# Tokens of experts 1 to 7 fetched by an indirect DMA and turned by transposes, in place of a gather by 0/1 products

## Chip, cores and metric

The kernel runs on one core of one Trainium2 chip. The metric is the device time of one execution in microseconds, lower is better. A comparison is made between medians of runs.

## What is computed

A two-layer decoder trunk on 256 tokens of width 1024, in float32. Layer 0 has two groups of sparse attention heads and a dense SwiGLU, layer 1 has stick-breaking attention and a top-2-of-8 expert SwiGLU. The part around the change is the last one:

```
logits = h @ w_router                       # h: 256 x 1024, normed tokens
top_v, top_i = top_k(logits, 2); top_w = softmax(top_v)
gates = sum(one_hot(top_i, 8) * top_w)      # 256 x 8, two non-zero a row
for e in range(8):                          # w_gate, w_up: 1024 x 3584, w_down: 3584 x 1024
    y = y + gates[:, e] * ((silu(h @ w_gate[e]) * (h @ w_up[e])) @ w_down[e])
```

All three matrices of all eight experts are read, 42 blocks of 1 MB for an expert, 336 in all.

## The kernel before

**Weights as a stream of units.** A unit is 1 MB of weights, 128 partitions x 2048 floats. SyncE loads units in a fixed order into a ring `raw` of R = 6 slots (L549), each load waiting until VectorE has finished with the slot's former unit (`lo_ready`). ScalarE copies a unit to `hi` in fp32r (L632), VectorE makes `lo = raw - hi` (L975), and TensorE takes each product three times, hi*hi, hi*lo and lo*hi (`three`, L1442 to L1444, 12 matmuls of 512 columns a unit). `hi` and `lo` have HM = 4 slots in the expert stage; ScalarE waits for `units_used` of TensorE to reuse one.

**Routing.** After the last norm (L997 writes the normed tokens into `work[:, 0:2]`), the router's logits are formed and VectorE finds each token's two experts. `rplace` is a token's place among the tokens of an expert, `rpick` says whether it was chosen. If no expert has over 128 tokens (`few`, read by each engine from `most_i`), the branch followed here runs; else a dense one over all tokens.

**Expert loop.** `make_place(e)` on VectorE (L1285) makes `place`, two 128x128 matrices (256 tokens in T = 2 blocks by 128 places) with a one where a token has a place. `gather(e)` on TensorE (L1837) forms the tokens of the expert with features on the partitions: for each of KD = 8 blocks of 128 features, four products of a block of the tokens (`xs_hi` and `xs_lo`, two blocks of tokens) with `place`, so 32 matmuls of 128 columns, into PSUM banks 4 and 5. ScalarE and VectorE copy them to `xg_hi` (L862) and `xg_lo` (L1294). `transpose_place(e)` (L1916) turns `place` for the scatter; ScalarE copies that to `placeT` (L905), and VectorE may then make the next `place`.

**Order within an expert**, as TensorE runs it (numbers are units, g, u and d are gate, up and down, c the chunk): g0 (0, 1), u0 (2, 3), g1 (4 to 7), u1 (8 to 11), d0 (12, 13), `transpose_place`, g2 (14 to 17), u2 (18 to 21), d1 (22 to 25), g3 (26 to 29), u3 (30 to 33), d2 (34 to 37), `gather(e + 1)`, d3 (38 to 41). Between them stand groups of four transposes of the hidden activations (`g_transpose_h`, L1908), whose input has a step of four floats, and the four scatter products of the expert before (L1853, L1854), into PSUM bank 6. Two such groups of transposes lie inside g2 and at its end, the seventh right behind `gather(e + 1)`. ScalarE's and VectorE's orders are written out to match, with splits of units ahead of what TensorE needs (to three units on ScalarE, two on VectorE). `few`, `gather` and the loop are printed below.

GpSimd makes constants at the start, applies masks in the attention stages and issues the loads of the norm gains (L598 to L602). It has no work after 478 us of the profile.

Of the kernel before, what the change touches and what calls it, by code (L numbers as in the profile page):

```python
# [20 lines left out]
F32 = mybir.dt.float32  # L21
# [5 lines left out]
P = 128  # L27
SEQ = 256
D = 1024
KD = D // P  # L30
T = SEQ // P
# [103 lines left out]
def build(nc, x_d, rel_bias, ev_norm_mix, ev_w_in, ev_kv_norm, ev_w_uk, ev_w_uv, ev_cmp_pos, ev_cmp_w1,  # L135
# [86 lines left out]
    buckets_d = nc.inline_tensor(bucket_rows(), "bucket_rows").ap()  # L222
    diag_d = nc.dram_tensor("bias_by_distance", [CH, SEQ + P], F32).ap()

    with ExitStack() as ctx:
        def sb(name, shape, dt=F32):
            return ctx.enter_context(nc.sbuf_tensor(name, shape, dt))

        def sem(name):
            return ctx.enter_context(nc.semaphore(name))  # L230
# [70 lines left out]
        before = sb("before", [P, P])  # L301
        place = sb("place", [P, T, P], F32R)
        placeT = sb("placeT", [P, SEQ], F32R)
        ones = sb("ones", [P, SEQ])
        root = sb("root", [P, 1])
        idle_sb = sb("idle_sb", [P, W], F32R)
# [25 lines left out]
        hd = nc.alloc_sbuf_tensor_at("hd", [P, T, D], F32, offset=arena_at)  # L332
        y_hi, y_lo = (h[:, 4:8, :].rearrange("p a s -> p (a s)") for h in (xT_hi, xT_lo))
        topw = kv[:, 0:SEQ]
        hankel = work[:, 2:4, :].rearrange("p a (b s) -> p (a b) s", s=SEQ)


# [83 lines left out]
        places_done = sem("places_done")  # L421
        count_ready = sem("count_ready")
        place_ready = sem("place_ready")
        gathered = sem("gathered")
        xg_hi_ready = sem("xg_hi_ready")
        xg_ready = sem("xg_ready")
# [134 lines left out]
        @block.gpsimd  # L561
        def _(pool):
            pool.memset(ident[:], 0.0).then_inc(ident_ready, 1)
            pool.memset(flip[:], 0.0).then_inc(flip_ready, 1)
            pool.wait_ge(ident_ready, 1)
            pool.affine_select(out=ident[:], in_=ident[:], compare_op=ALU.not_equal, fill=1.0, base=0,
                               pattern=[[-1, P]], channel_multiplier=1).then_inc(ident_ready, 1)
            pool.wait_ge(flip_ready, 1)
            pool.affine_select(out=flip[:], in_=flip[:], compare_op=ALU.not_equal, fill=1.0, base=-(P - 1),
                               pattern=[[1, P]], channel_multiplier=1).then_inc(flip_ready, 1)  # L570
            pool.iota(iota[:], [[1, P]], base=0, channel_multiplier=0, allow_small_or_imprecise_dtypes=True)\
                .then_inc(iota_ready, 1)
            pool.memset(before[:], 1.0).then_inc(iota_ready, 1)
            pool.wait_ge(iota_ready, 2)
            pool.affine_select(out=before[:], in_=before[:], compare_op=ALU.is_gt, fill=0.0, base=0,
                               pattern=[[1, P]], channel_multiplier=-1).then_inc(iota_ready, 1)

            pool.wait_ge(diag_copied, 1)
            pool.dma_start(diag_d, diag_sb[:]).then_inc(diag_stored, 16)
            pool.wait_ge(diag_stored, 16)  # L580
            pool.dma_start(hankel, bass.AP(tensor=diag_d.tensor, offset=diag_d.offset,
                                           ap=[[1, P], [SEQ + P, CH], [1, SEQ]])).then_inc(hankel_loaded, 16)

            pool.wait_ge(bias_copied, 4)
            pool.affine_select(out=bias_kT[:], in_=bias_kT[:], compare_op=ALU.is_ge, fill=NEG, base=P,
                               pattern=[[0, 8], [-1, SEQ]], channel_multiplier=1).then_inc(bias_masked, 1)

            pool.wait_ge(gates_ready, 1)
            pool.affine_select(out=gates[:, 0, 0:BH], in_=gates[:, 0, 0:BH], compare_op=ALU.is_ge, fill=0.0,
                               base=-(CMP_LEN - 1), pattern=[[0, BH]], channel_multiplier=1)\  # L590
                .then_inc(gates_masked, 1)
            for i, t in enumerate((1, 0)):
                pool.wait_ge(idx_summed, i + 1)
                n = P * (t + 1)
                pool.affine_select(out=iscore[:, t, 0:n], in_=iscore[:, t, 0:n], compare_op=ALU.is_ge, fill=UNSEEN,
                                   base=P * t, pattern=[[-1, n]], channel_multiplier=1).then_inc(idx_masked, 1)
            pool.wait_ge(xs_ready, 2)
            pool.dma_start(gain[:, 0, :], row_to_all(gains[2])).then_inc(gain_loaded[2], 16)  # L598
            pool.wait_ge(xs_ready, 4)
            pool.dma_start(gain[:, 1, :], row_to_all(gains[3])).then_inc(gain_loaded[3], 16)  # L600
            pool.wait_ge(xs_ready, 6)
            pool.dma_start(gain[:, 0, :], row_to_all(gains[4])).then_inc(gain_loaded[4], 16)  # L602


            for b in range(NSTICK + 1):
                if b < NSTICK:
                    n = P * (STICK[b][0] + 1)
                    pool.wait_ge(rest_ready, b + 1)
                    lt = logit_tile(b, n)[:, :, n - P:n]
                    pool.affine_select(out=lt, in_=lt, compare_op=ALU.is_gt, fill=1.0, base=0,  # L610
                                       pattern=[[0, 4], [-1, P]], channel_multiplier=1).then_inc(rest_masked, 1)
                if b:
                    n = P * (STICK[b - 1][0] + 1)
                    pool.wait_ge(sticks_done, b)
                    pt = prob_tile(b - 1, n)[:, :, n - P:n]
                    pool.affine_select(out=pt, in_=pt, compare_op=ALU.is_gt, fill=0.0, base=0,
                                       pattern=[[0, 4], [-1, P]], channel_multiplier=1).then_inc(stick_masked, 1)


        @block.scalar  # L620
        def _(act):
# [257 lines left out]
            def g_hT_high(e, s):  # L879
# [2 lines left out]
                act.activation(hT_hi[:, :, hT_slot(NSUB * e + s)], ps[:, 7, :].rearrange("p (j q) -> p j q", q=P),  # L882
                               ACT.Copy).then_inc(g_hT_hi_ready, 1)

            fits = few(act)
            with act.If(fits):
                done[0] = U_MOE + HM
# [74 lines left out]
        def _(dve):  # L962
# [362 lines left out]
                dve.tensor_tensor(hT_lo[:, :, dst], ps[:, 7, :].rearrange("p (j q) -> p j q", q=P),  # L1325
                                  hT_hi[:, :, dst].bitcast(F32), ALU.subtract).then_inc(g_hT_ready, 1)

            dve.wait_ge(iota_ready, 3)
            make_place(0)
            splits_to(U_MOE + HM)  # L1330
            fits = few(dve)
            with dve.If(fits):
                done[0] = U_MOE + HM
                gathered_low(0)
                for e in range(NE):
                    def used(k):

                        splits_to(min(first_of(e) + k + 2, U_END))

                    if e:  # L1340
                        used(0)
                        y_low(e - 1)
                    used(GATE_AT[1])
                    multiply(e, 0)
                    if e:
                        add_scattered(0, e - 1)
                    used(GATE_AT[1] + 2)
                    g_hT_low(e, 0)
                    if e:
                        add_scattered(1, e - 1)  # L1350
                    used(UP_AT[1])
                    if e:
                        add_scattered(2, e - 1)
                    used(UP_AT[1] + 2)
                    if e:
                        add_scattered(3, e - 1)
                    used(DOWN_AT[0])
                    multiply(e, 1)
                    used(GATE_AT[2])
                    if e + 1 < NE:  # L1360
                        dve.wait_ge(placeT_done, e + 1)
                        make_place(e + 1)
                    used(GATE_AT[2] + 2)
                    g_hT_low(e, 1)
                    used(UP_AT[2])
                    g_hT_low(e, 2)
                    used(DOWN_AT[1])
                    multiply(e, 2)
                    used(GATE_AT[3] + 2)
                    g_hT_low(e, 3)  # L1370
                    used(UP_AT[3])
                    g_hT_low(e, 4)
                    used(DOWN_AT[2])
                    multiply(e, 3)
                    used(DOWN_AT[2] + 2)
                    g_hT_low(e, 5)
                    used(DOWN_AT[3])
                    if e + 1 < NE:
                        gathered_low(e + 1)
                    g_hT_low(e, 6)  # L1380
# [55 lines left out]
        def _(pe):  # L1436
# [378 lines left out]

            keep_busy(14, 5)
            pe.wait_ge(picks_ready, 2)
            pe.wait_ge(iota_ready, 3)
            pk = [rpick[:, t, 0:NE] for t in range(T)]
            pe.matmul(ps[:, 4, 16:24], before[:], pk[0], start=True, stop=True)  # L1820
            pe.matmul(ps[:, 4, 24:32], before[:], pk[1], start=True, stop=False)
# [3 lines left out]

            def gather(e):

                pe.wait_ge(place_ready, e + 1)
                if e == 0:
                    pe.wait_ge(xs_lo_ready, 1)  # L1830
                else:
                    pe.wait_ge(g_silu_done, NCH * e)
                for k in range(KD):
                    out = ps[:, 4 + k // 4, P * (k % 4):P * (k % 4) + P]
                    for t in range(T):
# [75 lines left out]
            def transpose_place(e):  # L1911
# [4 lines left out]
                    ins = pe.transpose(ps[:, 6, P * t:P * t + P], place[:, t, :].bitcast(F32), ident[:])  # L1916
                ins.then_inc(placeT_done, 1)

            gather(0)
            keep_busy(22, 7)  # L1920
            fits = few(pe)
            with pe.If(fits):
                for e in range(NE):
# [19 lines left out]
                    g_transpose_h(e, 1, 1)  # L1943
                    gate(e, 2, 2, 3)
                    g_transpose_h(e, 2, 1)
                    up(e, 2, 0, 1, 2, 3)
                    down(e, 1, 0, 1, 2, 3)
                    gate(e, 3, 0, 1)
# [94 lines left out]
```

## Time and profile before

| | us |
|---|---|
| median of 3 runs | 1540.04 (1537.26 to 1540.17) |
| profiled execution, its own time | 1536.09 |
| its span, first to last instruction | 1534.3 |
| TensorE busy in the span | 1485.8 (97%) |
| VectorE busy | 1137.9 (74%) |
| ScalarE busy | 938.2 (61%) |
| GpSimd busy | 13.2 (1%) |
| mean granted clock of TensorE | 0.988 |

Busy times overlap between engines; an engine's idle time matters only where another that sets the end waits for it. The profiled execution is 3.95 us under the median and 1.8 us over its own span.

### The profile page before, as it was taken

How to read it: one execution, taken by the hardware profiler on the slowest of the kernel's cores; microseconds unless marked ns; L12 is line 12 of the kernel's file. 1: busy time of each engine (PE TensorE's matmuls, PEld its weight loads, DVE VectorE, ACT ScalarE, POOL GpSimd, SP SyncE). 2: the span in 40 equal slices, each digit the busy share in tenths (PEclk: the TensorE clock that was granted, in tenths of full speed). 3: DMA queues.
4: the chain of work that ended last, by engine and by line, in shares of the span. 5: the costliest groups of instructions: out<-in, count | busy, mean ns of one | idle time of the engine just before them, and what ended most of it. 6: DMA issues, size and time to landing. Idle time of an engine off the chain costs nothing.

```text
span 1534.3 us, 17550 instructions
## 1 busy us (share of the span) xinstructions
PE 1485.8 (97%) x7359; PEld 1252.5 (82%) x7359; DVE 1137.9 (74%) x841; ACT 938.2 (61%) x727; POOL 13.2 (1%) x28
## 2 busy tenths in 40 slices
PE   8998999999999799999999999999999999999996
PEld 7895788888887688888888888888888888888885
DVE  4586544544454688899888888889889979988885
ACT  4544344334343477777777767766767777776773
POOL 0000000000000000000000000000000000000000
PEclk9998999999999899999999999999999999999998
DMA  9732255563543379999999999999999999999991
GB/s 317 211 122 82 98 181 174 185 201 116 188 147 111 110 290 364 340 366 362 365 340 356 381 334 363 372 334 361 379 333 358 370 366 344 353 375 340 358 373 81
DMA packets 127603, 429.74 MB, mean 280 GB/s; under 512 B 11064, under 2 KB 20256, under 8 KB 111776
## 3 DMA queue, kind: packets, MB, share of 16 engines
q1 hardware_dynamic: 124320, 424.24, 76.6%
q0 software_dynamic: 736, 2.63, 0.5%
q10 hardware_dynamic: 2464, 1.69, 0.4%
q8 instruction: 60, 0.98, 0.3%
q14 instruction: 23, 0.19, 0.0%
HBM read 427.48 MB, written 1.06 MB: 279 GB/s over the span
## 4 chain that ended last, share of the span: by engine, by line
PE 91%; DVE 5%; ACT 2%; issue 1%; DMA 0%; POOL 0%; DVEq 0%; ACTq 0%; POOLq 0%
PE ps L1442 28%; PE ps L1444 28%; PE ps L1443 28%; PE ps L1837 2%; PE ps L1908 2%; DVE lo L975 1%; PE ps L1655 1%; DVE work L997 1%; PE ps L1501 1%; DMA x<-in_x_dram 0%; DVE kv L1054 0%; PE ps L1853 0%; ACT hi L632 0%; PE ps L1854 0%; DVE top L1053 0%
## 5 line engine op out<-in xcount | busy, mean ns | idle before, releaser
L975 DVE TENSOR_TENSOR lo<-raw,hi 128x2048 fp32r<-128x2048 f32 (+1 forms) x403 | 903.0, 2284 | 129.6 <-ACT hi L632 128.2
L632 ACT ACTIVATE hi<-raw 128x2048 fp32r<-128x2048 f32 (+1 forms) x403 | 770.5, 1915 | 282.1 <-PE ps L1444 276.9
L1442 PE MATMUL ps<-hi,xT_hi 128*128 128x512 f32 (+2 forms) x1216 | 473.4, 389 | 4.0 <-DVE xT_lo L1128 1.9
L1444 PE MATMUL ps<-hi,xT_lo 128*128 128x512 f32 (+2 forms) x1216 | 468.3, 385 | 0.0
L1443 PE MATMUL ps<-lo,xT_hi 128*128 128x512 f32 (+2 forms) x1216 | 467.9, 385 | 0.0
L1442 PEld LDWEIGHTS ps<-hi,xT_hi 128*128 128x128 f32 x1216 | 229.0, 188 | 49.7 <-issue 2.4
L1444 PEld LDWEIGHTS ps<-hi,xT_lo 128*128 128x128 f32 x1216 | 228.4, 188 | 46.6
L1443 PEld LDWEIGHTS ps<-lo,xT_hi 128*128 128x128 f32 x1216 | 228.7, 188 | 44.0
L1442 PE MATMUL ps<-hi,hT_hi 128*128 128x512 f32 x536 | 210.2, 392 | 0.9 <-DVE hT_lo L1178 0.9
L1444 PE MATMUL ps<-hi,hT_lo 128*128 128x512 f32 x536 | 208.8, 390 | 0.0
L1443 PE MATMUL ps<-lo,hT_hi 128*128 128x512 f32 x536 | 208.6, 389 | 0.0
L1442 PEld LDWEIGHTS ps<-hi,hT_hi 128*128 128x128 f32 x536 | 100.8, 188 | 21.5 <-DVE hT_lo L1178 1.1
L1444 PEld LDWEIGHTS ps<-hi,hT_lo 128*128 128x128 f32 x536 | 100.6, 188 | 21.1
L1443 PEld LDWEIGHTS ps<-lo,hT_hi 128*128 128x128 f32 x536 | 100.7, 188 | 20.4
L1325 DVE TENSOR_TENSOR hT_lo<-ps,hT_hi 128x512 fp32r<-128x512 f32 x56 | 38.7, 690 | 69.5 <-ACT hT_hi L882 69.5
L1442 PE MATMUL ps<-xT_hi,hi 128*128 128x256 f32 x248 | 71.3, 288 | 2.7 <-DVE xT_lo L1005 2.7
L1443 PE MATMUL ps<-xT_lo,hi 128*128 128x256 f32 x248 | 70.9, 286 | 0.0
L1444 PE MATMUL ps<-xT_hi,lo 128*128 128x256 f32 x248 | 70.8, 286 | 0.0
L882 ACT ACTIVATE hT_hi<-ps 128x512 fp32r<-128x512 f32 x56 | 33.4, 597 | 40.1 <-PE ps L1908 40.1
L1442 PEld LDWEIGHTS ps<-xT_hi,hi 128*128 128x128 f32 x248 | 48.2, 194 | 3.8 <-issue 3.6
L1444 PEld LDWEIGHTS ps<-xT_hi,lo 128*128 128x128 f32 x248 | 48.3, 195 | 0.0
L1443 PEld LDWEIGHTS ps<-xT_lo,hi 128*128 128x128 f32 x248 | 48.2, 194 | 0.0
(235 smaller groups left out, 932.7 us busy)
## 6 DMA issues: line engine op xcount, KB each, us to landing
raw<-in_od_w_gate_dram SPq DMA_DIRECT2D x112, 1024.0 KB, 7.3
raw<-in_od_w_up_dram SPq DMA_DIRECT2D x112, 1024.0 KB, 7.4
raw<-in_od_w_down_dram SPq DMA_DIRECT2D x112, 1024.0 KB, 7.4
raw<-in_od_w_qkv_dram SPq DMA_DIRECT2D x12, 1024.0 KB, 5.3
raw<-in_ev_w_gate_dram SPq DMA_DIRECT2D x11, 1024.0 KB, 6.2
raw<-in_ev_w_up_dram SPq DMA_DIRECT2D x11, 1024.0 KB, 5.1
raw<-in_ev_w_down_dram SPq DMA_DIRECT2D x11, 1024.0 KB, 5.1
raw<-in_ev_w_in_dram SPq DMA_DIRECT2D x4, 1024.0 KB, 10.5
```

The lines of the kernel that those rows point to most:

```text
L632: act.activation(unit(hi, n), unit(raw, n), ACT.Copy).then_inc(hi_ready, 1)
L882: act.activation(hT_hi[:, :, hT_slot(NSUB * e + s)], ps[:, 7, :].rearrange("p (j q) -> p j q", q=P), ACT.Copy).then_inc(g_hT_hi_ready, 1)
L975: dve.tensor_tensor(unit(lo, n), unit(raw, n), unit(hi, n).bitcast(F32), ALU.subtract)\
L997: dve.scalar_tensor_tensor(out=work[:, t, :], in0=x[:, t, :], scalar=stat[:, 2 + t:3 + t], in1=gain[:, i % 2, :], op0=ALU.mult, op1=ALU.mult)\
L1325: dve.tensor_tensor(hT_lo[:, :, dst], ps[:, 7, :].rearrange("p (j q) -> p j q", q=P), hT_hi[:, :, dst].bitcast(F32), ALU.subtract).then_in ...
L1442: pe.matmul(out, s_hi, m_hi, start=start, stop=False, skip_group_check=True)
L1443: pe.matmul(out, s_hi, m_lo, start=False, stop=False, skip_group_check=True)
L1444: return pe.matmul(out, s_lo, m_hi, start=False, stop=stop, skip_group_check=True)
L1501: pe.matmul(ps[:, bank, :], idle_sb[:, 0:P], idle_sb[:], start=True, stop=True)
L1655: ins = pe.matmul(ps[:, 6 + g % 2, :], val, probT[0:m, c].rearrange("p h q -> p (h q)"), start=(first and c == 0), stop=closes(b), skip_gr ...
L1837: ins = pe.matmul(out, part[:, t, P * k:P * k + P], place[:, t, :], start=(t == 0 and part is xs_hi), stop=(t == T - 1 and part is xs_lo))
L1908: ins = pe.transpose(ps[:, 7, P * j:P * j + P], work[:, 1, f + j:f + W:4], ident[:])
```

## The change

The normed tokens are stored once to DRAM (`normed_d`, 256 x 1024) from GpSimd's queue. For each expert from 1 to 7, TensorE multiplies `place` with a column of token numbers (two float32 products with one column), which gives the number of the token that has each place; VectorE copies these 128 numbers as integers to `picked`; GpSimd issues an indirect DMA that fetches the 128 rows of 4 KB into `rows`, which is `work[:, 2]`; and `gather(e)` becomes eight transposes of 128x128 of `rows`. A place without a token has number 0. Expert 0 is gathered as before.

```
+    normed_d = nc.dram_tensor("normed_tokens", [SEQ, D], F32).ap()
+        rows = work[:, 2, :]
 # GpSimd, at the start
+            pool.iota(token_id[:], [[P, T]], base=0, channel_multiplier=1, allow_small_or_imprecise_dtypes=True)\
+                .then_inc(iota_ready, 1)
 # GpSimd, after the masks of layer 1
+            pool.wait_ge(xs_ready, 8)
+            pool.dma_start(normed_d.rearrange("(t p) d -> p t d", p=P), work[:, 0:T, :]).then_inc(normed_stored, 16)
+            pool.wait_ge(normed_stored, 16)
+            fits = few(pool)
+            with pool.If(fits):
+                for e in range(1, NE):
+                    pool.wait_ge(picked_ready, e)
+                    if e > 1:
+                        pool.wait_ge(gathered, 2 * e)
+                    pool.indirect_dma_start(rows, None, normed_d, bass.IndirectOffsetOnAxis(ap=picked[:], axis=0))\
+                        .then_inc(rows_landed, 16)
 # ScalarE, before the expert loop
+            act.wait_ge(normed_stored, 16)
             fits = few(act)
 # VectorE, in the loop
                     used(UP_AT[2])
                     g_hT_low(e, 2)
+                    if e + 1 < NE:
+                        dve.wait_ge(picked_done, e + 1)
+                        if e:
+                            dve.wait_ge(rows_landed, 16 * e)
+                        dve.tensor_copy(picked[:], ps[:, 6, SEQ:SEQ + 1]).then_inc(picked_ready, 1)
                     used(DOWN_AT[1])
 # TensorE
             def gather(e):
-                pe.wait_ge(place_ready, e + 1)
-                if e == 0:
-                    pe.wait_ge(xs_lo_ready, 1)
-                else:
+                if e:
+                    pe.wait_ge(rows_landed, 16 * e)
                     pe.wait_ge(g_silu_done, NCH * e)
+                    for k in range(KD):
+                        ins = pe.transpose(ps[:, 4 + k // 4, P * (k % 4):P * (k % 4) + P], rows[:, P * k:P * k + P], ident[:])
+                        if k % 4 == 3:
+                            ins.then_inc(gathered, 1)
+                    return
+                pe.wait_ge(place_ready, 1)
+                pe.wait_ge(xs_lo_ready, 1)
                 for k in range(KD):
...
+            def pick_rows(e):
+
+                pe.wait_ge(place_ready, e + 1)
+                pe.wait_ge(placeT_ready, e)
+                for t in range(T):
+                    ins = pe.matmul(ps[:, 6, SEQ:SEQ + 1], place[:, t, :].bitcast(F32), token_id[:, t:t + 1],
+                                    start=(t == 0), stop=(t == T - 1))
+                ins.then_inc(picked_done, 1)
 # TensorE's loop
                     gate(e, 2, 2, 3)
                     g_transpose_h(e, 2, 1)
+                    if e + 1 < NE:
+                        pick_rows(e + 1)
                     up(e, 2, 0, 1, 2, 3)
```

TensorE and VectorE now wait for `iota_ready` at 4 where they waited for 3, since `token_id` is one more constant.

## Rows read from the trace of the kernel before

**Rows 1.** The page: span, busy time of three engines, and the slices of clock and DMA.
```profile
span 1534.3 us, 17550 instructions
...
PE 1485.8 (97%) x7359; PEld 1252.5 (82%) x7359; DVE 1137.9 (74%) x841; ACT 938.2 (61%) x727; POOL 13.2 (1%) x28
...
PEclk9998999999999899999999999999999999999998
DMA  9732255563543379999999999999999999999991
```

**Rows 2.** The page's chain that ended last, shares by engine.
```profile
PE 91%; DVE 5%; ACT 2%; issue 1%; DMA 0%; POOL 0%; DVEq 0%; ACTq 0%; POOLq 0%
```

**Rows 3.** Busy time by stretch: us, busy of each engine, PEclk, DMA share, GB/s.
```profile
560.00:1500.00 940.00, 940.00 (x4361) 785.56 (x4360) 819.50 (x468) 682.55 (x434) 0.00 (x0) 1.00 0.97 358
...
723.00:738.00 15.00, 15.00 (x69) 12.49 (x69) 12.19 (x7) 10.49 (x7) 0.00 (x0) 1.00 1.02 395
```

**Rows 4.** Waits between 560 and 1500 us: total, times, longest (the first and the last listed).
```profile
ACT hi L632 <- PE ps L1444: 159.9, 215, 1.3
...
DVE lo L975 <- ACT hi L632: 3.8, 9, 0.4
```

**Rows 5.** Chain in order of time, its long pieces: start, us, what.
```profile
765.33 3.52 PE ps L1837 x32
768.86 0.55 PE ps L1908 x4
797.09 0.47 PE ps L1908 x4
...
1382.80 3.52 PE ps L1837 x32
```

**Rows 6.** TensorE's timeline, float32 products with 8 columns: start, us.
```profile
517.42 0.39 PE L1820 MATMUL ps<-rpick,before 128*128 128x8 f32 x2 [2.34 <-DVE rgate L1273]
517.66 0.37 PE L1821 MATMUL ps<-rpick,before 128*128 128x8 f32 x2
...
518.33 0.47 PE L1824 MATMUL ps<-rpick,ones 128*128 128x8 f32 x2
```

**Rows 7.** TensorE's timeline where `place` is turned.
```profile
820.57 0.38 PE L1916 MATMUL ps<-ident,place 128*128 128x128 f32 x2
820.70 0.48 PE L1442 MATMUL ps<-hi,xT_hi 128*128 128x512 f32 x1
821.02 0.39 PE L1443 MATMUL ps<-lo,xT_hi 128*128 128x512 f32 x1
```

**Rows 8.** VectorE's timeline around a gather.
```profile
767.74 0.69 DVE L1294 TENSOR_TENSOR xT_lo<-ps,xT_hi 128x512 fp32r<-128x512 f32 x1 [2.12 <-ACT xT_hi L862]
769.52 0.69 DVE L1294 TENSOR_TENSOR xT_lo<-ps,xT_hi 128x512 fp32r<-128x512 f32 x1 [1.09 <-ACT xT_hi L862]
770.13 0.68 DVE L1325 TENSOR_TENSOR hT_lo<-ps,hT_hi 128x512 fp32r<-128x512 f32 x1
770.73 8.89 DVE L975 TENSOR_TENSOR lo<-raw,hi 128x2048 fp32r<-128x2048 f32 x4
```

**Rows 9.** TensorE's timeline at the end of g2: the third group of hidden transposes.
```profile
708.72 0.63 PE L1908 MATMUL ps<-ident,work 128*128 128x128 f32 x4
```

**Rows 10.** DMA issues: bytes each, median us from issue to landing.
```profile
raw<-in_od_w_gate_dram SPq DMA_DIRECT2D x112, 1024.0 KB, 7.3
...
work<-bias_by_distance POOLq DMA_DIRECT2D x1, 1024.0 KB, 9.5
out_dram<-work SPq DMA_DIRECT2D x2, 512.0 KB, 2.7
...
gain<-in_final_norm_dram POOLq DMA_DIRECT2D x1, 512.0 KB, 3.9
```

**Rows 11.** Timeline at the start of the expert stage, several engines.
```profile
502.69 2.48 DVE L997 SCALAR_TENSOR_TENSOR work<-x,stat,gain 128x1024 f32<-128x1024 f32 x2
...
534.92 0.39 PE L1442 MATMUL ps<-hi,xT_hi 128*128 128x512 f32 x1
```

More of the change, by code:

```diff
@@ L303, in build @@
         placeT = sb("placeT", [P, SEQ], F32R)
+        token_id = sb("token_id", [P, T])
+        picked = sb("picked", [P, 1], mybir.dt.uint32)
         ones = sb("ones", [P, SEQ])
@@ L423, in build @@
         place_ready = sem("place_ready")
+        normed_stored = sem("normed_stored")
+        picked_done = sem("picked_done")
+        picked_ready = sem("picked_ready")
+        rows_landed = sem("rows_landed")
         gathered = sem("gathered")
@@ L572, in _ @@
                 .then_inc(iota_ready, 1)
+            pool.iota(token_id[:], [[P, T]], base=0, channel_multiplier=1, allow_small_or_imprecise_dtypes=True)\
+                .then_inc(iota_ready, 1)
             pool.memset(before[:], 1.0).then_inc(iota_ready, 1)
-            pool.wait_ge(iota_ready, 2)
+            pool.wait_ge(iota_ready, 3)
             pool.affine_select(out=before[:], in_=before[:], compare_op=ALU.is_gt, fill=0.0, base=0,
@@ L1326, in g_hT_low @@
                                   hT_hi[:, :, dst].bitcast(F32), ALU.subtract).then_inc(g_hT_ready, 1)
-            dve.wait_ge(iota_ready, 3)
+            dve.wait_ge(iota_ready, 4)
             make_place(0)
@@ L1817, in _ @@
             pe.wait_ge(picks_ready, 2)
-            pe.wait_ge(iota_ready, 3)
+            pe.wait_ge(iota_ready, 4)
             pk = [rpick[:, t, 0:NE] for t in range(T)]
```

## The prediction, made before the changed kernel was timed

> **What bounds the kernel now.** I read the page first. TensorE is busy 97% of the span and its granted clock stands at 9 tenths or more in nearly every slice [rows 1]; the chain that ended last runs through TensorE for 91% [rows 2]. So the question is whether that holds in the expert stage, where the change sits. It does: between 560 and 1500 us TensorE is busy 940.00 of 940.00 us at clock 1.00 [rows 3]. Who waits for whom says the same: ScalarE's splits wait for TensorE 215 times, 159.9 us in all, and VectorE's splits wait for ScalarE only 3.8 us; no row of that stretch names a DMA [rows 4]. TensorE never sits idle there, so a microsecond taken out of its order should be a microsecond off the time, as long as nobody else becomes late.
>
> The chain in order of time has the gather as its longest piece, 3.52 us, and repeats it from 765.33 to 1382.80 us, six times [rows 5]. That gives the period of an expert: (1382.80 - 765.33) / 5 = 123.49 us.
>
> The second thing to see is how little the DMA has to spare. Its 16 engines are busy 0.97 of the stretch at 358 GB/s [rows 3]. An expert's weights are 42 loads of 1024.0 KB, 44.04 MB [rows 10], which over 123.49 us is 357 GB/s: the rate is that of the consumption. In a stretch in which VectorE freed slots quickly it reached 395 GB/s [rows 3], so 358 is not the ceiling, but the busy share is high at both rates.
>
> **The change, part by part.**
>
> *Removed.* 32 matmuls of 128 columns per expert for 7 experts: 3.52 us each [rows 5], 0.11 us a matmul. TensorE's order has nothing else in that piece.
>
> *Added in its place.* Eight transposes of 128x128 float32. The nearest rows are the groups of four on L1908: 0.47 us for four alone, 0.55 us right behind a gather [rows 5], so 0.12 to 0.14 us each, and the pair on L1916, after which the next-but-one matmul starts 0.45 us after the pair began, where two unit matmuls would have stood 0.23 apart without it: some 0.22 us for two [rows 7]. L1908 reads with a step of four floats, the new ones do not; they are also the same rate as the gather's own 0.11. Eight cost 0.88 (at 0.11) to 1.02 (twice 0.47, plus 0.08 for the following group). I take 0.90. Each of the removed and the added is one pass, so the gain is 3.52 - 0.90 = 2.62 us an expert.
>
> *Added: `pick_rows`, on TensorE's path.* Two float32 products with one column. The trace has five float32 products with eight columns, each recorded as two matmuls; they start 0.23 us apart (0.91 us from the first to the fifth) [rows 6]. Two cost 0.46. Bounds: 0.22 if they go like the pair in rows 7, and 0.94 if each stood alone with the whole 0.47 of the last one. I take 0.46. Their waits cost nothing: `placeT` and `place` come right after `transpose_place`, which is four units earlier, and a unit is 123.49 / 42 = 2.9 us. Behind `pick_rows` stands u2; if `place` were late, TensorE would stop there.
>
> *Added on VectorE.* One copy of 128x1, behind the third `hT_lo`. Its cost is under the 0.68 us of VectorE's 128x512 operations [rows 8], some 0.2 as I estimate; VectorE works 819.5 of 940 us [rows 3], so it lies beside TensorE. It waits for `picked_done`, which follows the third group of transposes by some 0.5 us, while VectorE itself must first get the copy of those transposes from ScalarE: no new wait. `rows_landed` of the expert before is long past. Behind the copy are the splits of u2's later units, which TensorE now never waits for.
>
> *Added on GpSimd and DMA.* The 128 rows are wanted by the gather at 765.2 us, and the pick runs about 709.3 us, behind the third transposes [rows 9, 5]: 56 us of cover. A direct load of 512 KB from GpSimd's queue landed 3.9 us after issue and the 1 MB one after 9.5 [rows 10]; the trace has no indirect one. With a copy and an issue of a microsecond each, even 9.5 us leaves 44 us. I take 0 for the path; the indirect form would have to take over 14 times the 3.9 us before TensorE waited, at the full excess for each of 7 experts. The `gathered` that GpSimd waits for lies more than 60 us back by then.
>
> What the fetch does to the weight stream is the real doubt. It adds 0.52 MB an expert. The period would be 123.49 - 2.62 + 0.46 = 121.33 us, the bytes 44.57 MB, the rate 367 GB/s. Against 395 GB/s there is 7% left; against a ceiling scaled from the average (358 / 0.97 = 369 GB/s) there is half a per cent. Loads land 7.3 us after issue with six slots of 2.9 us each, 17 us of ring, of which ScalarE and VectorE need some 5; so about 5 us of delay can build up before TensorE sees it, which one fetch of 0.52 MB (1.3 us at 395 GB/s) does not use. I take 0; the upper bound is a rival below.
>
> *The store and the waits at the start.* The store of 1 MB is issued when the last norm ends, 505.2 us, and should land in 5.4 (twice the 2.7 of the output's 512 KB) to 9.5 us [rows 10, 11], by 515. ScalarE's new wait comes behind its four splits, about 523 us, and TensorE's first unit is at 534.92 [rows 11]: covered by 8 us and more, cost 0. Were it later than 523, ScalarE's `gathered_high(0)` would be late, and dummy products up to 534.9 would still hide some 7 us. The extra iota is at the start, 500 us before use.
>
> *After the gather.* VectorE's copy of the first half waited 2.12 us for ScalarE and that for TensorE, the second 1.09 [rows 8]. With transposes both halves are there within 1.1 us, so VectorE's four splits from 770.73 move forward by nearly the 2.62 us that TensorE moves. Nothing new is late there.
>
> **Sum.** 7 x (3.52 - 0.90 - 0.46) = 7 x 2.16 = 15.1 us. Of the profiled execution's 1536.09 us that leaves 1521.0; that execution is 3.95 us under the median, so against 1540.04 it is 1524.9. By the bounds: best 7 x (3.52 - 0.88 - 0.22) = 16.9, worst 7 x (3.52 - 1.02 - 0.94) = 10.9. With 1.5 us on either side for where a median of three falls (they span 2.9), the forecast's own range is 1521.5 to 1530.5.
>
> **Rivals.**
>
> *A. The stream takes part of it back.* If the DMA tops out close to 369 GB/s, an expert needs 44.57 / 369 = 120.8 us of it, 0.5 us under the new period, and any unevenness now reaches TensorE. For it: the share of 0.97, and loads that land 7.3 us after issue when 1 MB alone at 395 GB/s takes 2.7. Against it: 395 GB/s over 15 us [rows 3], and a ring with some 5 us in hand. Half the gain lost: 1532; most of it lost: 1538, where it turns into no change.
>
> *B. The stream is already at its limit at 358 GB/s.* Then TensorE's order is worth nothing and the added bytes cost: 44.57 / 358 = 124.5 us an expert, 1.0 over the present 123.49, +7 us: 1547. For it: 358 in the long stretch, so even. Against it: TensorE has no idle time there, and 395 in the short one.
> The Trainium skill speaks for B: DMA: Bandwidth & Descriptors, section Bandwidth, gives about 358 GB/s as a core's share of its HBM and 425 for a core streaming alone. By the first figure the kernel would come out near 1547, by the second the stream needs 105 us an expert and does not matter. This trace has both 358 and 395, and the higher one can't be had under a limit of 358.
>
> *C. The rows go through one DMA engine, or two.* At 395 / 16 = 24.7 GB/s an engine needs 44.04 / 16 / 24.7 = 111.4 us for its part of an expert's weights; 0.52 MB more on one is 21.2 us, 132.6 in all, 9.1 us over 123.49: +64 us, 1604. It decides from the point at which the busiest engine gets more than 121.3 - 111.4 = 9.9 us of rows, that is with two engines or fewer. For it: nothing shown, the form is new to this trace. Against it: the direct loads of the same 128 x 4 KB landed in 3.9 us [rows 10], which one engine could not do.
>
> **Chances.** Forecast 0.80; A 0.11 (of it 0.03 at no change); B 0.04; C and late rows in any other way 0.03; the remaining 0.02 is a gain beyond the best bound. Under 0.2% (3 us) this measurement can hardly tell a change from none. Faster 0.90, same 0.03, slower 0.07. The range takes the forecast's own and A down to half the gain: 1519.5 to 1532.5.
>
> **What would show it.** In the changed profile: L1837 only 32 products, all before 530 us; the new transposes as pieces of about 0.9 us in the chain; the picks in 0.46; a period of 121.3 us; TensorE still busy in all of 560 to 1480; fetches landing within 10 us of issue. Wrong would be: rows of waits in which ScalarE's splits wait for a DMA (A, B), a DMA share at 1.0 with TensorE idle, TensorE waiting at the transposes for `rows_landed` (C), or loads whose landing grows beyond 12 us.

## The result and the profile after

The changed kernel takes 1522.66 us (median of 4 runs, 1521.9 to 1523.24) against 1538.88 us for the kernel before in the same comparison (4 runs): ratio 0.9894, 95% interval 0.988 to 0.9908, 16.2 us less. The forecast was 1524.9 us and 15.1 us less, against the 1540.04 us that the kernel before had then. The profiled execution took 1522.32 us, its span is 1520.2 us.

First the page, the lines that answer to [rows 1, 2]:

```profile
span 1520.2 us, 17311 instructions
...
PE 1470.7 (97%) x7219; PEld 1237.5 (81%) x7219; DVE 1137.7 (75%) x848; ACT 936.9 (62%) x727; POOL 33.4 (2%) x37
...
PE 90%; DVE 5%; ACT 2%; issue 1%; DMA 0%; ACTq 0%; POOL 0%; DVEq 0%; POOLq 0%
```

TensorE is busy for 15.1 us less, which is most of what the time fell by; GpSimd has 20 us more, which nobody waits for.

The chain in order of time, its long pieces in the expert stage (L1861 are the new transposes, L1942 is L1908 of before):

```profile
764.98 0.87 PE ps L1861 x8
765.86 0.48 PE ps L1942 x4
...
1371.15 0.87 PE ps L1861 x8
1372.02 0.48 PE ps L1942 x4
```

Where [rows 5] have a piece of 3.52 us there is one of 0.87 us, and the group of transposes behind it costs 0.48 in place of 0.55. The period (the time from one expert's gather to the next one's) is (1371.15 - 764.98) / 5 = 121.23 us; it was 123.49. TensorE's timeline at the end of g2, the same place as [rows 9]:

```profile
707.92 0.63 PE L1942 MATMUL ps<-ident,work 128*128 128x128 f32 x4
708.39 0.50 PE L1958 MATMUL ps<-token_id,place 128*128 128x1 f32 x4
708.75 0.48 PE L1471 MATMUL ps<-hi,xT_hi 128*128 128x512 f32 x1
```

From the start of the four transposes to the next unit it is 0.83 us. In the kernel before the transposes began at 708.72 us [rows 9], and the next unit followed after 0.39 us:

```profile
709.11 0.48 PE L1442 MATMUL ps<-hi,xT_hi 128*128 128x512 f32 x1
```

So the picks take 0.44 us of TensorE's order. Busy time by stretch, to be held against [rows 3]:

```profile
560.00:1480.00 920.00, 920.00 (x4202) 765.97 (x4202) 815.29 (x473) 679.00 (x432) 19.25 (x7) 1.00 0.99 368
```

TensorE is still busy in every microsecond, at clock 1.00, while the stream has gone from 358 to 368 GB/s and the DMA engines from 0.97 to 0.99. Who waits for whom between 560 and 1480 us, against [rows 4]:

```profile
ACT hi L655 <- PE ps L1473: 160.0, 218, 1.3
...
ACT hi L655 <- DMA raw<-in_od_w_gate_dram: 0.9, 1, 0.9
ACT hi L655 <- DMA raw<-in_od_w_up_dram: 0.7, 1, 0.7
```

For the first time two of ScalarE's splits wait for a load, by under 1 us each. No matmul waits for it: TensorE has no idle time in these 920 us. GpSimd's timeline and the DMA issues show the fetch itself:

```profile
589.47 2.80 POOL L639 DMA_INDIRECT work<-normed_tokens,picked  x1 [81.91 <-DVE picked L1395]
710.69 2.76 POOL L639 DMA_INDIRECT work<-normed_tokens,picked  x1 [118.42 <-DVE picked L1395]
```

```profile
raw<-in_od_w_gate_dram SPq DMA_DIRECT2D x112, 1024.0 KB, 7.7
...
normed_tokens<-work POOLq DMA_DIRECT2D x1, 1024.0 KB, 4.4
...
work<-normed_tokens,picked POOLq DMA_INDIRECT x7, 10.1
```

An indirect fetch holds GpSimd for 2.8 us and lands 10.1 us after issue, not the 3.9 us of a direct load of the same bytes [rows 10]; it is issued at 710.7 and wanted at 764.8 us. The store landed in 4.4 us.

### The profile page after: what moved, and what is told of

It is laid out like the page before. It is cut to its first block, busy times and chain, and to the rows that moved or that the text cites. A ratio compares the mean times of both kernels' runs of the same rounds, so it can differ in the third digit from the quotient of the medians.

```text
span 1520.2 us, 17311 instructions
## 1 busy us (share of the span) xinstructions
PE 1470.7 (97%) x7219; PEld 1237.5 (81%) x7219; DVE 1137.7 (75%) x848; ACT 936.9 (62%) x727; POOL 33.4 (2%) x37
## 4 chain that ended last, share of the span: by engine, by line
PE 90%; DVE 5%; ACT 2%; issue 1%; DMA 0%; ACTq 0%; POOL 0%; DVEq 0%; POOLq 0%
PE ps L1471 28%; PE ps L1473 28%; PE ps L1472 28%; PE ps L1942 2%; DVE lo L999 1%; PE ps L1684 1%; PE ps L1530 1%; DVE work L1021 1%; ACT hi L655 1%; DMA x<-in_x_dram 0%; PE ps L1871 0%; DVE kv L1078 0%; PE ps L1887 0%; PE ps L1888 0%; PE ps L1861 0%
## 5 line engine op out<-in xcount | busy, mean ns | idle before, releaser
L999 DVE TENSOR_TENSOR lo<-raw,hi 128x2048 fp32r<-128x2048 f32 (+1 forms) x403 | 902.9, 2283 | 129.8 <-ACT hi L655 128.3
## 6 DMA issues: line engine op xcount, KB each, us to landing
raw<-in_ev_w_in_dram SPq DMA_DIRECT2D x4, 1024.0 KB, 10.1
```

What stands on the lines that cost most here:

```text
L999: dve.tensor_tensor(unit(lo, n), unit(raw, n), unit(hi, n).bitcast(F32), ALU.subtract)\
```

## The experiments

The period of an expert can be read from each trace to 0.02 us where TensorE never waits, which no median of whole runs can do: executions of one kernel differed by 1.3 to 2.9 us in the first comparison and by up to 8 us in the last one (1536.11 to 1544.28 us for the kernel before). So the verdicts below rest on the period unless a ratio is given.

### Is the fetch free in the stream? One, two, four and eight fetches an expert

Fetches after the first go into space that is unused in this branch, so the gathers still read the same rows. VectorE overwrites `picked` only when the extra ones have landed too; `one_fetch` leaves out GpSimd's wait for `gathered` and waits on VectorE for the one fetch.

```
-                for e in range(1, NE):                                   # one_fetch
+                for e in range(1, 2):
...
-                    pe.wait_ge(rows_landed, 16 * e)
+                    pe.wait_ge(rows_landed, 16)
...
+                    for k in range(N - 1):                               # fetch_x2, x4, x8: N = 2, 4, 8
+                        if k % 4 == 0 and (extra := (N - 1) * (e - 1) + k):
+                            pool.wait_ge(spare_landed, 16 * extra)
+                        pool.indirect_dma_start(spare[:, k % 4, :], None, normed_d,
+                                                bass.IndirectOffsetOnAxis(ap=picked[:], axis=0))\
+                            .then_inc(spare_landed, 16)
```

> The rows are fetched for expert 1 alone; experts 2 to 7 compute with expert 1's rows, so the output differs. Everything on TensorE stays, picks and transposes too. Theory (TensorE sets the period, the fetch is free): period from transposes to transposes 121.2 us as with seven fetches (121.23), span within 2 us of 1520.2. Rival A (the weight stream takes part of the gain back): the period falls below 121.2, since 0.52 MB of 44.57 an expert are gone; at most to 120.9.

> Each expert's rows are fetched twice, the second time into unused space: 45.1 MB an expert, 372 GB/s at a period of 121.23 us. Theory, with a ceiling of the stream near 395 GB/s: period 121.2. Rival A with a ceiling of 369 GB/s: 45.1 / 369 = 122.2 us, span longer by 7.

> Four fetches an expert, three of them into unused space: 46.1 MB, 381 GB/s at a period of 121.23 us. Theory: period 121.2 to 121.5. Rival A (369 GB/s): 125.0 us, span longer by 26.

> Eight fetches an expert, seven of them into unused space: 48.2 MB, 398 GB/s at a period of 121.23 us. Theory, ceiling 395: 122.1 us, so the first sign of TensorE waiting, span longer by some 6. Rival A (369 GB/s): 130.7 us, span longer by 66. If neither shows, the ceiling is above 398.

The chain of `one_fetch`, the first and last of its eight transposes between 766 and 1374 us:

```profile
766.92 0.87 PE ps L1859 x8
...
1373.09 0.87 PE ps L1859 x8
```

(1373.09 - 766.92) / 5 = 121.23 us: without the fetch the period is the same to 0.01 us. The stream gives nothing back, so it had taken nothing from TensorE.

`fetch_x2`, the same rows:

```profile
767.15 0.87 PE ps L1870 x8
...
1373.32 0.87 PE ps L1870 x8
```

121.23 us again. `fetch_x4`, busy time by stretch (us, busy of TensorE, its weight load, VectorE, ScalarE, GpSimd, clock, DMA share, GB/s), the second of 40 us behind one expert's four fetches, and two of its waits between 560 and 1480 us:

```profile
700.00:1480.00 780.00, 780.00 (x3565) 649.42 (x3564) 690.90 (x401) 574.32 (x368) 50.59 (x24) 1.00 1.00 381
720.00:760.00 40.00, 40.00 (x181) 33.26 (x180) 34.98 (x19) 29.07 (x18) 1.65 (x1) 1.00 1.02 413
```

```profile
ACT hi L663 <- PE ps L1482: 122.1, 167, 1.3
ACT hi L663 <- DMA raw<-in_od_w_gate_dram: 33.2, 22, 3.2
```

Its period, (1372.81 - 766.60) / 5, is 121.24 us. ScalarE now waits for loads 22 times and up to 3.2 us for gate weights alone, the DMA share reads 1.00, and TensorE is still busy in all 780 us at 381 GB/s. So a ceiling of 369 GB/s is refuted (it asked for 125.0 us), and so is one of 358. Nor is 395 one: 413 GB/s went through in 40 us, and TensorE never waited. `fetch_x8` is where it breaks:

```profile
700.00:1480.00 780.00, 756.40 (x3395) 624.44 (x3394) 659.59 (x386) 545.72 (x350) 84.00 (x48) 0.99 1.00 379
```

```profile
ACT hi L663 <- DMA raw<-in_od_w_up_dram: 37.1, 21, 3.2
PEld ps L1480 <- DVE lo L1007: 30.6, 16, 4.5
PE ps L1480 <- DVE lo L1007: 27.5, 19, 4.0
```

The period is 126.4 to 128.9 us, the span 1565.9. Here the delay comes all the way through: load, ScalarE, VectorE, TensorE. I had said 122.1 and rival A 130.7; neither holds.

The mean of 379 GB/s is no ceiling of the stream. One expert of this run in four stretches, from the first issue on, shows when TensorE waits:

```profile
718.86:738.86 20.00, 20.00 (x90) 16.56 (x89) 17.37 (x9) 12.27 (x7) 9.37 (x5) 1.00 0.97 371
738.86:748.86 10.00, 10.00 (x48) 8.34 (x47) 6.46 (x4) 6.23 (x4) 4.46 (x3) 1.00 1.03 412
748.86:768.86 20.00, 16.27 (x64) 12.67 (x63) 14.95 (x9) 13.51 (x9) 0.00 (x0) 0.91 1.02 419
768.86:846.29 77.43, 77.43 (x359) 64.55 (x358) 69.03 (x45) 57.10 (x39) 0.00 (x0) 1.00 0.99 367
```

TensorE is idle only in the third stretch, while 419 GB/s go through, and busy throughout the last 77 us at 367 GB/s. It is so for all seven experts: in the 20 us that begin 30 us behind the first issue TensorE is busy 16.0 to 17.1 us at 412 to 420 GB/s, and outside it TensorE is idle for only 0.3 and 1.1 us, with two of the experts, just before it. The eight fetches come within 34 us, and in the 50 us from the first issue they and the weights at TensorE's pace (44.04 MB in 121.23 us, 363 GB/s) would need about 447 GB/s, an estimate from these numbers. So the burst overran the ring; what eight fetches cost when they are spread over the period was not tried.

### How much cover does the fetch need? Picks two units ahead of the gather

```
                     g_transpose_h(e, 2, 1)
-                    if e + 1 < NE:
-                        pick_rows(e + 1)
...
                     g_transpose_h(e, 5, 3)
+                    if e + 1 < NE:
+                        pick_rows(e + 1)
                     down(e, 2, 2, 3)
```

VectorE's copy moves behind the sixth `hT_lo` in the same way.

> The picks, the copy and so the fetch move from behind the third group of hidden transposes to behind the sixth, two units (5.4 us) ahead of the gather in place of 57 us. Theory: the fetch is free only because of its cover. It takes 10.1 us from issue to landing, plus about 2 us from the picks to the issue, so TensorE now waits some 6 us at the gather for each of 7 experts: period 127, span longer by about 45. Rival (the fetch's 10.1 us is mostly queueing behind weight loads, which are fewer when TensorE stands still): wait 1 to 3 us, period 122 to 124.

TensorE's and GpSimd's timelines of `late_pick`, at the picks and at the gather:

```profile
768.16 0.50 PE L1958 MATMUL ps<-token_id,place 128*128 128x1 f32 x4
...
779.82 1.97 PE L1861 MATMUL ps<-ident,work 128*128 128x128 f32 x8 [5.57 <-DMA work<-normed_tokens,picked]
781.58 1.06 PE L1942 MATMUL ps<-ident,work 128*128 128x128 f32 x4
```

```profile
770.02 2.76 POOL L639 DMA_INDIRECT work<-normed_tokens,picked  x1 [126.36 <-DVE picked L1405]
```

And the stretches around it:

```profile
774.00:780.00 6.00, 0.43 (x3) 0.18 (x2) 0.14 (x1) 0.00 (x0) 0.00 (x0) 0.81 0.98 345
780.00:784.00 4.00, 4.00 (x16) 3.71 (x16) 2.08 (x4) 2.52 (x4) 0.00 (x0) 0.50 0.39 151
784.00:788.00 4.00, 4.00 (x18) 3.20 (x18) 4.00 (x3) 2.65 (x2) 0.00 (x0) 0.94 0.18 16
```

From the picks to the issue it is 1.9 us and from issue to landing 9.8, and TensorE waits 5.57 us here, 5.7 us on average over the seven gathers (5.0 to 7.4), as the sum had it (6). The period is 129.1 us, though, the mean of six that run from 128.3 to 131.3: 7.9 more than 121.23 and not 6. After the idle the granted clock is at 0.50, which is 1.2 GHz, from 780 to 784 us, and the eight transposes take 1.97 us in place of the 1.03 us they have in the changed kernel, from their first start to their last end. The rest of 7.9 - 5.7 = 2.2 us is that slower stretch. A stall here costs about 1.4 times its length.

The landing did not get shorter while TensorE stood still. The rival is not refuted by that, since its condition did not come about: the DMA share was 0.98 from 774 to 780 us, so the weight loads ran on. Whether the 10 us are the fetch's own or queueing behind weight loads, no run here shows.

### The picks by themselves

`products_with_fetch` keeps the gather by 32 products and adds picks, copy and fetch; the fetched rows are not used.

```
-                if e:
+                pe.wait_ge(place_ready, e + 1)
+                if e == 0:
+                    pe.wait_ge(xs_lo_ready, 1)
+                else:
                     pe.wait_ge(rows_landed, 16 * e)
                     pe.wait_ge(g_silu_done, NCH * e)
-                    for k in range(KD):
-                        ins = pe.transpose(ps[:, 4 + k // 4, P * (k % 4):P * (k % 4) + P], rows[:, P * k:P * k + P], ident[:])
-                        if k % 4 == 3:
-                            ins.then_inc(gathered, 1)
-                    return
-                pe.wait_ge(place_ready, 1)
-                pe.wait_ge(xs_lo_ready, 1)
```

> The kernel before with the picks, the copy and the fetches added; the gather is still 32 products and the fetched rows are not used. Theory: the period is that of before, 123.49 us, plus the picks' 0.44: 123.9. If the fetch had a price of its own in the stream, more than that.

Its chain:

```profile
643.74 3.52 PE ps L1867 x32
...
1387.41 3.52 PE ps L1867 x32
```

(1387.41 - 643.74) / 6 = 123.945 us, 0.455 over 123.49, so the picks cost 0.46 us an expert and the fetch adds nothing of its own. The transposes in place of products therefore save 123.945 - 121.23 = 2.71.

`pick_fp32r`:

```
-        token_id = sb("token_id", [P, T])
+        token_id = sb("token_id", [P, T, 2])
+        token_r = sb("token_r", [P, T, 2], F32R)
...
-                    ins = pe.matmul(ps[:, 6, SEQ:SEQ + 1], place[:, t, :].bitcast(F32), token_id[:, t:t + 1],
+                    ins = pe.matmul(ps[:, 6, SEQ:SEQ + 2], place[:, t, :], token_r[:, t, :],
```

> The picks as fp32r products with two equal columns in place of float32 ones with one. A float32 product is recorded as two matmuls, an fp32r one as one, so two matmuls in place of four. Theory (every matmul of a pick costs its 0.11 us on TensorE's path): period 121.23 - 0.22 = 121.0, span 1.5 us shorter. Rival (the picks' cost is a fixed change-over): no change.

TensorE's timeline of it, then its chain:

```profile
709.02 0.63 PE L1945 MATMUL ps<-ident,work 128*128 128x128 f32 x4
709.41 0.36 PE L1962 MATMUL ps<-token_r,place 128*128 128x2 f32 x2
709.63 0.47 PE L1474 MATMUL ps<-hi,xT_hi 128*128 128x512 f32 x1
```

```profile
765.87 0.87 PE ps L1864 x8
...
1370.94 0.87 PE ps L1864 x8
```

Two matmuls in 0.22 us (0.61 us from the transposes to the unit, less the 0.39 without picks) where there were four in 0.44; the period is (1370.94 - 765.87) / 5 = 121.01, 0.22 less. The cost goes with the number of matmuls, and no fixed change-over shows in it.

### The start of the loop, and a faster version

In the profile of the changed kernel the first unit of the loop began at 536.36 us and not at 534.92 as in [rows 11], although expert 0 is gathered as before. Four runs on one chip asked what that is and timed the improved picks.

> The kernel before, once more, to see how far two executions of one kernel part. Theory: the period of an expert is the same to 0.02 us (123.49), and where the expert loop begins moves by 1 to 3 us from one execution to the next, by the DMA-bound steps of the first 50 us; the 1.4 us by which the changed kernel's profile began its loop later is such a difference. Rival: the change delays the start itself; then this run begins its loop near 534.9 us again.

> The changed kernel, timed in more rounds beside the others of this call. Theory: 7 x (123.49 - 121.23) = 15.8 us faster than before, ratio 0.9897.

> Picks as fp32r products with two columns. The period was 121.01, so 7 x 0.22 = 1.5 us below the changed kernel and 17.4 below before, ratio 0.9887. With a spread of 1 to 3 us between runs the difference to the changed kernel may stay inside the interval.

> As pick_fp32r, and the 22 dummy products between the gather of expert 0 and the first unit are 6. They take 7.2 us from 529.2 us on, while the operands of the first unit are there by some 531. Theory: the first units start some 4 us earlier, partly at the lower clock: 2 to 4 us less, ratio 0.986. Rival: without the filler the clock stays at 1.2 GHz longer, or VectorE's splits are not ahead yet, and nothing is won or a few us are lost.

The edit of `short_filler`, beside that of `pick_fp32r`:

```
             gather(0)
-            keep_busy(22, 7)
+            keep_busy(6, 7)
```

TensorE's timeline of `before_again`, then of `short_filler`:

```profile
537.49 0.39 PE L1442 MATMUL ps<-hi,xT_hi 128*128 128x512 f32 x1
```

```profile
531.69 2.75 PE L1533 MATMUL ps<-idle_sb 128*128 128x512 f32 x6
534.28 0.40 PE L1474 MATMUL ps<-hi,xT_hi 128*128 128x512 f32 x1
534.51 0.39 PE L1475 MATMUL ps<-lo,xT_hi 128*128 128x512 f32 x1
```

The kernel before, once more, began its loop at 537.49 us, 2.6 us later than in its first profile, with its span 2.6 us longer (1536.9) and the period unchanged (767.90 to 1385.36 us for five, 123.49). So executions of one kernel differ there by more than the 1.4 us in question. From the start of the loop to the end of the span it is 999.4 us in both profiles of the kernel before (1534.3 - 534.92 and 1536.9 - 537.49), and 983.8 and 983.5 us in the two of the changed kernel (1520.2 - 536.36 and 1521.9 - 538.38), 15.7 us less. What the medians differ by beyond that, 0.5 us more in the first comparison (16.2) and 1.5 us less in this one (14.2), lies mostly ahead of the loop and has no constant sign. A delay of under 1 us by the change is not excluded. Where the difference arises is not shown: ScalarE's first split began at 20.63 us in the changed kernel's profile, at 19.31 in the first one of the kernel before and at 19.74 in `before_again`, whose loop began last of the three.

| | us, median | ratio to before, 95% interval |
|---|---|---|
| kernel before (11 runs) | 1538.29 | |
| changed kernel (6) | 1524.06 | 0.9901, 0.9879 to 0.9923 |
| with fp32r picks (5) | 1521.02 | 0.9878, 0.9855 to 0.9901 |
| and 6 dummy products (4) | 1516.92 | 0.9853, 0.9826 to 0.988 |

In `short_filler` the units start 2.6 us behind the end of the gather, in place of 7.2 in the changed kernel's profile, and already at their spacing of 0.23 us, so the operands were there, and the other 16 dummy products bought nothing. I had expected the first units partly at the lower clock; they were not, and the median fell by 4.1 us against the picks as fp32r products, a little beyond the 2 to 4 given. It is the fastest of the versions, 21.4 us under the kernel before. The step from the changed kernel to fp32r picks is shown by the period, which gives 1.5 us; the medians differ by 3.0, and their two intervals overlap. The intervals of the last two rows overlap as well, though none of their executions do (1515.56 to 1519.01 against 1519.22 to 1522.1 us).

## Why the prediction was right, step by step

- **TensorE bounds the expert stage.** Right: 940 of 940 us before, 920 of 920 after, and the time fell by TensorE's own work: 7 x (123.49 - 121.23) = 15.8 us. The forecast of 15.1 was 0.7 short of that; the medians fell by 16.2 us and, in the second comparison, by 14.2. Of the 2.2 us between 1524.9 and the measured 1522.66, 1.2 are that the kernel before itself came out at 1538.88 and not 1540.04, which the prediction could not know.
- **Transposes for products.** The forecast was 3.52 - 0.90 = 2.62 us, measured 2.71 (`products_with_fetch` against the changed kernel). The piece is 0.87 us where I took 0.90, and the group behind it is 0.07 us shorter. I had counted the 0.08 us by which a group behind a gather is dearer only in the upper bound, not as something the change would give back. These two are the missing 0.1 us, 0.6 us of the total.
- **The picks.** Taken 0.46, measured 0.455 by the period and 0.44 on the timeline. The row of float32 products with eight columns was the right one: what counts is the number of matmuls (four), and one column costs what eight do.
- **The fetch off the path.** Right, for the reason given (cover, the time from issue to need, of some 54 us against a landing of 10.1), and `late_pick` shows that it is the cover: with two units of it TensorE waits. The landing was estimated from direct loads at 3.9 to 9.5 us; it is 10.1, just outside, and also beyond the 10 us that I had named as a sign of being right, at no cost here.
- **Room in the stream.** Right that there is room, shown by one, two and four fetches with one period. The bounds were both too low. 395 GB/s, read from a stretch of 15 us, was passed by 413 GB/s over 40 us in `fetch_x4`. And 369, which is 358 / 0.97, takes the busy share to grow with the rate: it read 0.97 at 358 GB/s, 1.00 at 381 and 1.02 at 413. The sum also went by means over a period, while a fetch comes as a burst; that did no harm with one fetch and set the time with eight. The changed kernel needs 368.
- **Rivals.** A and B are refuted by `fetch_x4` (381 GB/s, no idle). One sign that I had listed for them did appear, ScalarE's splits waiting for a load (1.6 us in all), and so it was badly chosen: in `fetch_x4` such waits come to 54.5 us and TensorE loses nothing. The Trainium skill's figure of about 358 GB/s for a core's share of HBM, DMA: Bandwidth & Descriptors, section Bandwidth, which is for two cores of a pair that both stream, does not bound this core, which runs alone: 381 GB/s over 780 us is above it. C, the rows through one DMA engine or two, does not occur: through one a fetch would take 21 us by the prediction's rate, and it lands in 10. Through two it would take 10.6, which the landing alone does not exclude, but four such fetches would put 42 us on top of these engines' 111.4 us for the weights, 154 us an expert, and the period of `fetch_x4` is 121.24.
- **Store and start.** The store landed in 4.4 us, below the 5.4 to 9.5 given; that the start is delayed by the change is not seen, to within 1 us or so.

## What to carry to other kernels

Where one engine is busy in every microsecond of a stage, look for work that an idle queue could take: here it was gained in full. The period of the loop in the trace tells such a gain to a hundredth of a microsecond when whole runs scatter by three to eight. Multiply the moved transfer until the time changes, which shows how far its room goes: here four times is free and eight times is not. Then look by stretch where the waiting starts, since the mean rate can hide a burst: the run with eight fetches moved 379 GB/s on average and 419 where TensorE waited. And count what a late transfer costs twice, as the wait and as the slower clock behind it.

## What the runs showed of the hardware

- An indirect DMA of 128 rows of 4 KB holds GpSimd for 2.74 to 2.80 us when none stands right before it (0.9 to 1.9 us for most of those that follow at once in `fetch_x8`). It lands in 8.2 us (`products_with_fetch`, stream of 361 GB/s) to 11.6 us (`late_pick`, 344 GB/s), 10.1 us in the median of the changed kernel.
- The DMA share in the profile does not grow in step with the rate, and a share of 1.00 does not mean that the consumer waits: it read 0.97 at 358 GB/s (kernel before), 0.99 at 368 (changed kernel), 1.00 at 381 and 1.02 at 413 (`fetch_x4`), and TensorE was never idle in any of these.
- One core's weight stream with fetches beside it moved 412 to 420 GB/s over 20 us (`fetch_x8`).
- After idles of 5.0 to 7.4 us in `late_pick` TensorE's granted clock fell; in the 4 us behind the idle it was 0.50 to 0.65 on average. An idle of 5.7 us on average made the period 7.9 us longer.
- A float32 product whose moving operand has one column costs TensorE 0.22 us, two matmuls; an fp32r one with two columns 0.11.
